# Splitting the mixer's weight pieces once and keeping both parts in DRAM, in a hybrid attention and retention layer

## The chip, the cores and the metric

The kernel runs on one core of a Trainium2 chip. The metric is device time in microseconds (us), as the median of the runs of one kernel. A core has TensorE (PE, matmuls; PEld is its weight load), VectorE (DVE), ScalarE (ACT), GpSimd (POOL) and SyncE (SP), which here only issues transfers; its 16 DMA engines are shared by all queues.

## What is computed

One step of one decoder layer, in fp32, for a prompt of 1024 tokens and a sample group of 8 sequences of 8 tokens that share the weights:

```
x = LN(alpha*x + 0.5 * swiglu(x, ffn_wi[0], ffn_wo[0]))          # D_MODEL 1024, D_FF 2816
q_a,k_a,v_a,q_r,k_r,v_r,g_r,gate_a,gate_b = split(x @ w_in)
o_a = sliding_window_attention(rope(q_a), rope(k_a), v_a)        # window 128, sinks, caches
o_r = group_norm(retention(rope(q_r), rope(k_r), v_r)) * silu(g_r)
m = sigmoid(gate_a) * (o_a @ w_br_attn) + sigmoid(gate_b) * (o_r @ w_br_ret)
x = LN(alpha*x + m @ w_o)
x = LN(alpha*x + 0.5 * swiglu(x, ffn_wi[1], ffn_wo[1]))
```

The middle four lines are the mixer. Besides the two activations the outputs are the new key and value caches and the retention states.

## The kernel before, in words

**Three parts.** The first feed-forward block runs to about 718 us, the mixer to about 1692 us, the second feed-forward block to the end. The activations stay in SBUF, partly spilled to DRAM.

**Precision.** An fp32 product is made of three matmuls (`three`, L2228 to L2232; `token_major`, L2504 and L2505, for outputs with tokens on the partitions): high part by high part, high by low, low by high. So every operand exists as a high part (rounded, type fp32r) and a low part (operand minus high part).

**The mixer's order.** `TIMELINE` (`build_timeline`, L100) is one list of stages for three token groups (G = 0, 1, 2): groups 0 and 1 have 384 prompt tokens each, group 2 has 256 and the 64 sample rows. Per retention head there are P (projection), PVQ, G and G2, TR (transposes of the rotated q and k), SKV, GN, B; then KVA and QA for the attention, gates GB and GA with the sigmoids SGB and SGA, attention units AS, EX, AP, AV, FIN, the product A with `w_br_attn`, WO (product with `w_o`), and in group 2 also the stages of the sample rows (KC reads the cached keys, SP, SV, SU). Every engine walks the same list.

**Weight pieces.** The weights of the mixer are cut into 66 pieces of 128 x 1024 (`NP_PHASE`), the same 66 in each group, so 198 in all (`NPIECES`). `STAGE_PIECES` (L167) says how many pieces a stage reads: four for P and QA, two for B, KVA and WO, else one. B and WO wait for both pieces together and free both at their end, the other stages take one after the other. A piece goes through these steps, in every group anew:

- SP loads 512 KB into one of `RAW` = 3 raw slots (`load_piece`, L721), in one transfer or a few, with rows of up to 4 KB, once the split of the piece that was there before is done.
- ACT copies it to the high part in one of `MSLOTS` = 4 slots (`split_hi`, L507 to L513), after the load and after PE has used the piece that was in the slot (`piece_used`).
- DVE computes the low part, raw minus high (`split_lo`, L515 to L520).
- PE waits for `lo_ready` and reads both parts (L2230 and L2232 the high part, L2231 the low part).

**Who sets the order.** ACT's and DVE's instruction order is written out by the code: class `Pace` (L626) puts the splits between the other work of the stages, some pieces ahead of the stage that reads them. The other work of DVE in the mixer is the rope (L1892 and on, ending in the tiles `qk` at L1940), the low parts of operands, masks and norms; that of ACT is copies out of PSUM, exponentials and sigmoids (L1282), the copy of `probT` (L1336). SP's queue holds the loads of the pieces in order (loop at L747); behind them wait the first loads of the second block's weights (`load_a`), the spills of `y` and then the rest of the second block (`ffn(1)`). The cached keys and values are loaded by POOL in group 2 (L941 and L943). The semaphores `x_loaded` belong to the input tiles of the first block and are waited for again at L1752, L1753 and L1790.

Of the kernel before, what the change touches and what calls it, by code (L numbers as in the profile page):

```python
# [13 lines left out]
P = 128  # L14
# [177 lines left out]
def slot_of(n):  # L192

    return n % MSLOTS


# [103 lines left out]
def hybrid_layer(nc, w, c, o):  # L300
# [4 lines left out]
    with ExitStack() as ctx:  # L305
# [110 lines left out]
        raw = stack("raw", RAW * D)  # L416
        w_hi4, w_lo4 = stack("w_hi4", MSLOTS * D, FR), stack("w_lo4", MSLOTS * D, FR)
        xg_hi, xg_lo = stack("xg_hi", KT * TG, FR), stack("xg_lo", KT * TG, FR)
# [9 lines left out]
        h_d = nc.dram_tensor("h_spill", (P, KD, PRODS, 512), F32, kind="Internal").ap()  # L428
        y_d = nc.dram_tensor("y_spill", (P, NT, D), F32, kind="Internal").ap()


# [11 lines left out]
        x11_loaded, x12_loaded, x21_loaded, x22_loaded, a11_loaded = x_loaded[0:4], x_loaded[4:6], x_loaded[6], x_loaded[7], x_loaded[8]  # L443
        xst_loaded = sem("xst_loaded")
        xs_done, xs_act, xs_dve = sem("xs_done"), sem("xs_act"), sem("xs_dve")
        u_hi_ready, u_dve, prod_done = sem("u_hi_ready"), sem("u_dve"), sem("prod_done")
# [41 lines left out]
        def wslot(n, lo):  # L488
            s = slot_of(n)
            return (w_lo4 if lo else w_hi4)[:, s * D:(s + 1) * D]  # L490

# [5 lines left out]
        def fr(ap):  # L497
            return ap.bitcast(F32)
# [8 lines left out]
        def split_hi(eng, n):  # L507

            eng.wait_ge(raw_loaded[n % RAW], RAW_AT[n])
            if n >= MSLOTS:  # L510
                eng.wait_ge(piece_used, n - MSLOTS + 1)
            s = n % RAW
            nc.scalar.activation(wslot(n, False), raw[:, s * D:(s + 1) * D], ACT.Copy).then_inc(hi_ready, 1)  # L513
# [112 lines left out]
        class Pace:  # L626
# [4 lines left out]
            def upto(self, n):  # L631
                while self.n < min(n, NPIECES):
                    self.split(self.eng, self.n)
                    self.n += 1
# [15 lines left out]
        def _(sp):  # L650
# [70 lines left out]
            def load_piece(n):  # L721
# [3 lines left out]
                for width, off, src in sources[n]:  # L725
                    k, cols = src.shape[1], src.shape[2]
                    dst = raw[:, s * D:(s + 1) * D].rearrange("p (k n) -> p k n", n=width)[:, 0:k, off:off + cols]
                    sp.dma_start(dst, src).then_inc(raw_loaded[s], 16)

            def load_xt(dst, feats, toks, k0, nk, landed):  # L730
                src = w["x_prompt_t"][feats * HALF + k0 * P:feats * HALF + (k0 + nk) * P, toks * HALF:(toks + 1) * HALF]
                sp.dma_start(dst[:, k0 * HALF:(k0 + nk) * HALF].rearrange("p (k c) -> p k c", k=nk),
                             src.rearrange("(k p) c -> p k c", p=P)).then_inc(landed, 16)
# [12 lines left out]
            ffn(0)  # L746
            for n in range(RAW, NPIECES):  # L747
                load_piece(n)
            sp.wait_ge(st_stored, 16 * HR)
            sp.wait_ge(out_stored, 16 * (2 + HR + 2 + 2 * DB))  # L750
# [642 lines left out]
        def _(dve):  # L1393
# [345 lines left out]
            def product_evac(f, q):  # L1739
                if q == 1:  # L1740
                    last_y.clear()
                for i in range(4):
                    src = bank(down_bank(q, i))
                    product_done(f, q, i)
                    if q == 1:
                        dve.wait_ge(tile_out, 28 * f + 4)
                        tt(part(c11, i), part(u_sum, i), src, ALU.add).then_inc(tile_out, 1)
                    elif q in (2, 5):
                        dve.wait_ge(tile_out, 28 * f + 4 * q)
                        tt(part(u_sum, i), part(u_sum, i), src, ALU.add).then_inc(tile_out, 1)  # L1750
                    elif q == 3:
                        dve.wait_ge(x_loaded[i], 32 + 16 * f)  # L1752
                        dve.wait_ge(x_loaded[i + 4], 32 + 16 * f)  # L1753
                        y_add(i, 1, ALPHA, src)
                        y_out(f, q, i + 4, 1, ALPHA, src)
                    elif q == 4:
                        y_out(f, q, i, 1, 1.0, src)
                    elif q == 6:
                        y_out(f, q, i + 4, 0, 1.0, src)
# [28 lines left out]
            def sample_out(f, half):  # L1788
                t = NT - 1
                dve.wait_ge(x_loaded[t], 32 + 16 * f)  # L1790
                dve.wait_ge(fold8_done, 2 * f + half + 1)
                stt(y_half(t, half), y_half(t, half), ALPHA, bank(7, SR), ALU.mult, ALU.add).then_inc(y8_out, 1)
# [432 lines left out]
        def _(pe):  # L2225
# [266 lines left out]
            def token_major(n, npieces, kper, width, b0, G, first=0, tile=None):  # L2492

                for i in range(first, first + npieces):
                    pe.wait_ge(lo_ready, n + i + 1 - first)
                    wh, wl = wslot(n + i - first, False), wslot(n + i - first, True)
# [17 lines left out]
            def gate(n, b, G):  # L2514
                TGn = tokens_of(G)
                pe.wait_ge(lo_ready, n + 1)
                wh, wl = wslot(n, False), wslot(n, True)
# [5 lines left out]
            for kind, G, x, n in TIMELINE:  # L2523
# [121 lines left out]
                elif kind == "B":  # L2645
                    pe.wait_ge(lo_ready, n + 2)
                    pe.wait_ge(or_lo_ready, g + 1)
# [139 lines left out]
                elif kind == "A":  # L2787
                    pe.wait_ge(lo_ready, n + 1)
                    if x == 0:
# [13 lines left out]
                elif kind == "WO":  # L2803
                    pe.wait_ge(lo_ready, n + 2)
                    pe.wait_ge(m_lo_ready, 4 * G + x + 1)
# [133 lines left out]
```

## Time and profile before

| | |
|---|---|
| median of 3 runs | 2414.72 us (2413.87 to 2414.76) |
| the profiled execution | 2422.92 us |
| its span | 2421.1 us |
| granted TensorE clock, mean | 0.994 |
| busy share PE, DVE, ACT, POOL | 98%, 69%, 38%, 9% |
| moved by DMA | 300.04 MB, 124 GB/s in the mean |

The trace is that of one execution, which took 8.2 us longer than the median. Busy shares are means over the whole span; a stretch has its own. A time in brackets behind an instruction is the idle time of its engine just before it, with what ended it. In the rows by stretch each engine has its busy microseconds and its number of instructions, then come the granted clock, the busy share of the 16 DMA engines and the GB/s they moved. Where several transfers overlap, that share can be above 1.

### The profile page before, as it was taken

What the parts mean: (1) busy time and instruction counts of PE and PEld (TensorE: products, weight loads), DVE (VectorE), ACT (ScalarE), POOL (GpSimd) and SP (SyncE); (2) the same over time, 40 slices, a digit from 0 to 9 for tenths busy, and PEclk for the clock granted to TensorE, in tenths of its full rate; (3) what the DMA queues carried; (4) which work ended last, traced back from release to release, by engine and by line L of the source; (5) the groups of instructions that cost most, each with busy time, mean ns of one, the idle gap of its engine ahead of it and who ended that gap; (6) DMA issues with size and microseconds to landing.
All of it is one profiled execution on the core that took longest, in us unless ns stands there. A gap on an engine that the chain in (4) does not pass through costs nothing.

```text
span 2421.1 us, 30917 instructions
## 1 busy us (share of the span) xinstructions
PE 2383.4 (98%) x12165; PEld 2027.9 (84%) x12165; DVE 1673.2 (69%) x2340; ACT 910.5 (38%) x1347; POOL 211.5 (9%) x297
## 2 busy tenths in 40 slices
PE   8999999999999999999999999999999999999997
PEld 7888888887888998989999778888788888888786
DVE  8666666656887657666666767577866666665788
ACT  5222222343444337443356333373422222234344
POOL 4000000000111000000100111202300000000011
PEclk9999999999999999999999999999999999999999
DMA  5222223276443334343342445534222222327643
GB/s 167 92 99 96 100 91 106 96 227 195 148 142 115 121 96 118 98 129 105 107 116 89 139 136 168 169 97 148 75 96 83 96 100 89 107 95 228 204 146 129
DMA packets 227857, 300.04 MB, mean 124 GB/s; under 512 B 14465, under 2 KB 167345, under 8 KB 224881
## 3 DMA queue, kind: packets, MB, share of 16 engines
q1 hardware_dynamic: 213392, 239.91, 32.0%
q0 software_dynamic: 13056, 56.48, 6.4%
q8 instruction: 97, 1.59, 0.3%
q10 hardware_dynamic: 1264, 1.67, 0.2%
q14 instruction: 48, 0.39, 0.0%
HBM read 243.81 MB, written 55.18 MB: 123 GB/s over the span
## 4 chain that ended last, share of the span: by engine, by line
PE 89%; DVE 6%; DMA 2%; ACT 2%; issue 1%; SPq 0%; ACTq 0%; POOL 0%; DVEq 0%
PE ps L2230 26%; PE ps L2231 25%; PE ps L2232 25%; PE ps L2349 3%; DMA b_raw<-in_ffn_wo 2%; PE ps L2438 1%; PE ps L2439 1%; DVE b_lo L1563 1%; DMA raw<-in_w_in 1%; PE ps L2604 1%; DVE w_lo L519 1%; PE ps L2739 1%; PE ps L2716 1%; DVE y L1429 1%; PE ps L2616 0%
## 5 line engine op out<-in xcount | busy, mean ns | idle before, releaser
L2230 PE MATMUL ps<-xc_hi,u_both 128*128 128x512 f32 x1240 | 485.9, 392 | 7.7 <-DVE u_both L1621 6.2
L2232 PE MATMUL ps<-xc_hi,u_both 128*128 128x512 f32 x1240 | 483.6, 390 | 0.0
L2231 PE MATMUL ps<-xc_lo,u_both 128*128 128x512 f32 x1240 | 483.5, 390 | 0.0
L519 DVE TENSOR_TENSOR w_lo<-raw,w_hi 128x1024 fp32r<-128x1024 f32 x198 | 238.8, 1221 | 103.5 <-ACT w_hi L513 103.2
L2230 PEld LDWEIGHTS ps<-xc_hi,u_both 128*128 128x128 f32 x1240 | 233.5, 188 | 56.3 <-DVE u_both L1621 6.2
L2232 PEld LDWEIGHTS ps<-xc_hi,u_both 128*128 128x128 f32 x1240 | 233.3, 188 | 49.0
L2231 PEld LDWEIGHTS ps<-xc_lo,u_both 128*128 128x128 f32 x1240 | 233.4, 188 | 47.9
L513 ACT ACTIVATE w_hi<-raw 128x1024 fp32r<-128x1024 f32 x198 | 205.4, 1054 | 163.6 <-PE ps L2232 93.5
L2230 PE MATMUL ps<-b_hi,h_hi 128*128 128x512 f32 x616 | 242.1, 393 | 4.3 <-DVE b_lo L1563 4.3
L2231 PE MATMUL ps<-b_lo,h_hi 128*128 128x512 f32 x616 | 240.5, 390 | 0.0
L2232 PE MATMUL ps<-b_hi,h_lo 128*128 128x512 f32 x616 | 240.4, 390 | 0.0
L2230 PE MATMUL ps<-w_hi,xg_hi 128*128 128x256 f32 (+1 forms) x640 | 219.7, 343 | 0.0
L2231 PE MATMUL ps<-w_lo,xg_hi 128*128 128x256 f32 (+1 forms) x640 | 215.5, 337 | 0.0
L2232 PE MATMUL ps<-w_hi,xg_lo 128*128 128x256 f32 (+1 forms) x640 | 215.4, 337 | 0.0
L1112 ACT ACTIVATE h_hi<-h_raw 128x512 fp32r<-128x512 f32 x154 | 97.3, 632 | 273.2 <-PE ps L2232 160.0
L1523 DVE TENSOR_TENSOR u_both<-wa,u_both 128x1024 fp32r<-128x1024 f32 x84 | 104.8, 1248 | 94.4 <-ACT u_both L986 94.4
L986 ACT ACTIVATE u_both<-wa 128x1024 fp32r<-128x1024 f32 (+1 forms) x89 | 93.3, 1048 | 197.6 <-PE ps L2349 100.4
L986 ACT ACTIVATE u_both<-ws 128x1024 fp32r<-128x1024 f32 x63 | 66.8, 1060 | 233.5 <-PE ps L2232 140.6
L1562 DVE TENSOR_TENSOR h_lo<-h_raw,h_hi 128x512 fp32r<-128x512 f32 x154 | 105.7, 686 | 64.3 <-ACT b_hi L986 64.0
L2230 PEld LDWEIGHTS ps<-b_hi,h_hi 128*128 128x128 f32 x616 | 116.0, 188 | 34.5 <-DVE b_lo L1563 8.5
L2232 PEld LDWEIGHTS ps<-b_hi,h_lo 128*128 128x128 f32 x616 | 116.0, 188 | 24.4
L2231 PEld LDWEIGHTS ps<-b_lo,h_hi 128*128 128x128 f32 x616 | 116.0, 188 | 23.6
(352 smaller groups left out, 4421.8 us busy)
## 6 DMA issues: line engine op xcount, KB each, us to landing
raw<-in_w_in SPq DMA_DIRECT2D x90, 512.0 KB, 3.9
wa<-in_ffn_wi SPq DMA_DIRECT2D x87, 512.0 KB, 3.8
h_raw<-h_spill SPq DMA_DIRECT2D x154, 256.0 KB, 2.9
h_spill<-tm POOLq DMA_DIRECT2D x22, 1024.0 KB, 4.2
b_raw<-in_ffn_wo SPq DMA_DIRECT2D x66, 256.0 KB, 3.9
raw<-in_w_in SPq DMA_DIRECT2D x96, 128.0 KB, 2.5
raw<-in_w_in SPq DMA_DIRECT2D x48, 256.0 KB, 3.3
raw<-in_w_br_ret SPq DMA_DIRECT2D x24, 512.0 KB, 4.4
```

Source lines behind the costliest of these rows:

```text
L513: nc.scalar.activation(wslot(n, False), raw[:, s * D:(s + 1) * D], ACT.Copy).then_inc(hi_ready, 1)
L519: nc.vector.tensor_tensor(wslot(n, True), raw[:, s * D:(s + 1) * D], fr(wslot(n, False)), ALU.subtract).then_inc(lo_ready, 1)
L986: nc.scalar.activation(dst, src, ACT.Copy).then_inc(sem_, 1)
L1112: nc.scalar.activation(h_hi[s][:], h_raw[s][:], ACT.Copy)
L1429: return nc.vector.scalar_tensor_tensor(out=out, in0=in0, scalar=scalar, in1=in1, op0=op0, op1=op1)
L1523: tt(u_lo[s][:], w_src[i][:], fr(u_hi[s][:]), ALU.subtract).then_inc(u_dve, 1)
L1562: tt(h_lo[s][:], h_raw[s][:], fr(h_hi[s][:]), ALU.subtract)
L1563: tt(b_lo[s][:], step_source(q, k, s), fr(b_hi[s][:]), ALU.subtract).then_inc(d_lo_ready, 1)
L2230: mm(out, a_hi, b_hi, start=first, stop=False)
L2231: mm(out, a_hi, b_lo, start=False, stop=False)
L2232: return mm(out, a_lo, b_hi, start=False, stop=last)
L2349: ins = mm(out, xs[:, k * P:(k + 1) * P], both[:, k], start=first and k == 0, stop=last and k == 3)
```

## The change

The splits are made in group 0 only. A slot holds both parts of a piece side by side, [high | low], 8 KB on each partition. In group 0 SP stores each split piece as 1 MB to a DRAM tensor `w_split` (`store_piece`), three loads behind; ACT's `split_hi` waits for the store of the piece that was in its slot before. In groups 1 and 2 SP fetches high and low part together, 1 MB, into the slot (`fetch_piece`) once PE has used what was there, and PE waits for `piece_fetched` in the place of `lo_ready`. `SPLIT_IN` maps a piece of group 1 or 2 to the piece of group 0 with the same weights. The stores and fetches count on eight of the semaphores `x_loaded`, so the waits of the second block on them get new values (`x_landed`).

```diff
--- before.py
+++ after.py
@@ -194,6 +194,31 @@
     return n % MSLOTS
 
 
+FIRST_USE = {(kind, x, i): n + i for kind, G, x, n in TIMELINE if G == 0 for i in range(STAGE_PIECES.get(kind, 0))}
+SPLIT_IN = {n + i: FIRST_USE[kind, x, i] for kind, G, x, n in TIMELINE
+            if kind in STAGE_PIECES and n >= NP_PHASE for i in range(STAGE_PIECES[kind])}
+
+
+def stored_count(n):
+
+    return 16 * (n // MSLOTS + 1)
+
+
+def fetched_count(n):
+
+    return 16 * sum(u % MSLOTS == n % MSLOTS for u in range(NP_PHASE, n + 1))
+
+
+def x_landed(t, f):
+
+    pieces = 0
+    if t < MSLOTS:
+        pieces = sum(n % MSLOTS == t for n in range(NP_PHASE))
+    elif t < 2 * MSLOTS:
+        pieces = sum(n % MSLOTS == t - MSLOTS for n in range(NP_PHASE, NPIECES))
+    return 32 + f * 16 * (1 + pieces)
+
+
 def block_order():
 
     return [(ci, p) for kind, p in HEAD for ci in {"E": EARLY, "L": LATE, "U": ()}[kind]]
@@ -414,7 +439,7 @@
         tA, tB = stack("tA", 512), stack("tB", 512)
         sig = stack("sig", KT * TG)
         raw = stack("raw", RAW * D)
-        w_hi4, w_lo4 = stack("w_hi4", MSLOTS * D, FR), stack("w_lo4", MSLOTS * D, FR)
+        w_both4 = stack("w_both4", MSLOTS * 2 * D, FR)
         xg_hi, xg_lo = stack("xg_hi", KT * TG, FR), stack("xg_lo", KT * TG, FR)
         ret_mask = stack("ret_mask", HR * P)
         ret_mask_s = stack("ret_mask_s", HR * SR)
@@ -427,6 +452,7 @@
 
         h_d = nc.dram_tensor("h_spill", (P, KD, PRODS, 512), F32, kind="Internal").ap()
         y_d = nc.dram_tensor("y_spill", (P, NT, D), F32, kind="Internal").ap()
+        w_d = nc.dram_tensor("w_split", (NP_PHASE, P, 2 * D), F32, kind="Internal").ap()
 
 
         raw_loaded = [sem(f"raw_loaded{i}") for i in range(RAW)]
@@ -442,6 +468,7 @@
         xb_sum, xb_done, xb_hi, xb_lo = [sem(n) for n in ("xb_sum", "xb_done", "xb_hi", "xb_lo")]
         x11_loaded, x12_loaded, x21_loaded, x22_loaded, a11_loaded = x_loaded[0:4], x_loaded[4:6], x_loaded[6], x_loaded[7], x_loaded[8]
         xst_loaded = sem("xst_loaded")
+        piece_stored, piece_fetched = x_loaded[0:MSLOTS], x_loaded[MSLOTS:2 * MSLOTS]
         xs_done, xs_act, xs_dve = sem("xs_done"), sem("xs_act"), sem("xs_dve")
         u_hi_ready, u_dve, prod_done = sem("u_hi_ready"), sem("u_dve"), sem("prod_done")
         s1_ready, q_ready, c11_ready, u3_ready, u2_ready, u1_ready, c12_ready = [
@@ -487,7 +514,14 @@
 
         def wslot(n, lo):
             s = slot_of(n)
-            return (w_lo4 if lo else w_hi4)[:, s * D:(s + 1) * D]
+            return w_both4[:, (2 * s + lo) * D:(2 * s + lo + 1) * D]
+
+        def wait_piece(eng, n):
+
+            if n < NP_PHASE:
+                eng.wait_ge(lo_ready, n + 1)
+            else:
+                eng.wait_ge(piece_fetched[slot_of(n)], 32 + fetched_count(n))
 
         def wait_affine(eng, k, t):
 
@@ -509,6 +543,7 @@
             eng.wait_ge(raw_loaded[n % RAW], RAW_AT[n])
             if n >= MSLOTS:
                 eng.wait_ge(piece_used, n - MSLOTS + 1)
+                eng.wait_ge(piece_stored[slot_of(n)], 32 + stored_count(n - MSLOTS))
             s = n % RAW
             nc.scalar.activation(wslot(n, False), raw[:, s * D:(s + 1) * D], ACT.Copy).then_inc(hi_ready, 1)
 
@@ -629,7 +664,7 @@
                 self.eng, self.split, self.n = eng, split, start
 
             def upto(self, n):
-                while self.n < min(n, NPIECES):
+                while self.n < min(n, NP_PHASE):
                     self.split(self.eng, self.n)
                     self.n += 1
 
@@ -727,6 +762,19 @@
                     dst = raw[:, s * D:(s + 1) * D].rearrange("p (k n) -> p k n", n=width)[:, 0:k, off:off + cols]
                     sp.dma_start(dst, src).then_inc(raw_loaded[s], 16)
 
+            def store_piece(n):
+                s = slot_of(n)
+                sp.wait_ge(lo_ready, n + 1)
+                sp.dma_start(w_d[n], fr(w_both4[:, 2 * s * D:2 * (s + 1) * D])).then_inc(piece_stored[s], 16)
+
+            def fetch_piece(n):
+                s, m = slot_of(n), SPLIT_IN[n]
+                sp.wait_ge(piece_used, n - MSLOTS + 1)
+                if n - MSLOTS < NP_PHASE:
+                    sp.wait_ge(piece_stored[s], 32 + stored_count(n - MSLOTS))
+                sp.wait_ge(piece_stored[slot_of(m)], 32 + stored_count(m))
+                sp.dma_start(fr(w_both4[:, 2 * s * D:2 * (s + 1) * D]), w_d[m]).then_inc(piece_fetched[s], 16)
+
             def load_xt(dst, feats, toks, k0, nk, landed):
                 src = w["x_prompt_t"][feats * HALF + k0 * P:feats * HALF + (k0 + nk) * P, toks * HALF:(toks + 1) * HALF]
                 sp.dma_start(dst[:, k0 * HALF:(k0 + nk) * HALF].rearrange("p (k c) -> p k c", k=nk),
@@ -744,8 +792,13 @@
             load_a(0, 0, 2)
             load_a(0, 0, 3)
             ffn(0)
-            for n in range(RAW, NPIECES):
+            for n in range(RAW, NP_PHASE):
                 load_piece(n)
+                store_piece(n - RAW)
+            for n in range(NP_PHASE - RAW, NP_PHASE):
+                store_piece(n)
+            for n in range(NP_PHASE, NPIECES):
+                fetch_piece(n)
             sp.wait_ge(st_stored, 16 * HR)
             sp.wait_ge(out_stored, 16 * (2 + HR + 2 + 2 * DB))
             sp.wait_ge(m_ready, KT * NG)
@@ -1749,8 +1802,8 @@
                         dve.wait_ge(tile_out, 28 * f + 4 * q)
                         tt(part(u_sum, i), part(u_sum, i), src, ALU.add).then_inc(tile_out, 1)
                     elif q == 3:
-                        dve.wait_ge(x_loaded[i], 32 + 16 * f)
-                        dve.wait_ge(x_loaded[i + 4], 32 + 16 * f)
+                        dve.wait_ge(x_loaded[i], x_landed(i, f))
+                        dve.wait_ge(x_loaded[i + 4], x_landed(i + 4, f))
                         y_add(i, 1, ALPHA, src)
                         y_out(f, q, i + 4, 1, ALPHA, src)
                     elif q == 4:
@@ -1787,7 +1840,7 @@
 
             def sample_out(f, half):
                 t = NT - 1
-                dve.wait_ge(x_loaded[t], 32 + 16 * f)
+                dve.wait_ge(x_loaded[t], x_landed(t, f))
                 dve.wait_ge(fold8_done, 2 * f + half + 1)
                 stt(y_half(t, half), y_half(t, half), ALPHA, bank(7, SR), ALU.mult, ALU.add).then_inc(y8_out, 1)
 
@@ -2492,7 +2545,7 @@
             def token_major(n, npieces, kper, width, b0, G, first=0, tile=None):
 
                 for i in range(first, first + npieces):
-                    pe.wait_ge(lo_ready, n + i + 1 - first)
+                    wait_piece(pe, n + i - first)
                     wh, wl = wslot(n + i - first, False), wslot(n + i - first, True)
                     for kk in range(kper):
                         k = i * kper + kk
@@ -2513,7 +2566,7 @@
 
             def gate(n, b, G):
                 TGn = tokens_of(G)
-                pe.wait_ge(lo_ready, n + 1)
+                wait_piece(pe, n)
                 wh, wl = wslot(n, False), wslot(n, True)
                 for k in range(KT):
                     ins = three(bank(b, n=TGn), wh[:, k * P:(k + 1) * P], wl[:, k * P:(k + 1) * P],
@@ -2643,7 +2696,8 @@
                                                       ident[0:R, 0:R])
                     ins.then_inc(t_done, 1)
                 elif kind == "B":
-                    pe.wait_ge(lo_ready, n + 2)
+                    wait_piece(pe, n)
+                    wait_piece(pe, n + 1)
                     pe.wait_ge(or_lo_ready, g + 1)
                     for f in range(KT):
                         if f in (1, 2):
@@ -2785,7 +2839,7 @@
                                          probT[:, q * P + b4 * 32:q * P + (b4 + 1) * 32], start=False, stop=(b4 == 3))
                     ins.then_inc(av_done, 1)
                 elif kind == "A":
-                    pe.wait_ge(lo_ready, n + 1)
+                    wait_piece(pe, n)
                     if x == 0:
                         pe.wait_ge(oa_lo_ready, 3 * G + 3)
                         pe.wait_ge(pT_ready, 6 * G + (6 if not last_group else 5))
@@ -2801,7 +2855,8 @@
                                         oaT_hi[:, k * TG:k * TG + TGn], oaT_lo[:, k * TG:k * TG + TGn], k == 0, k == 3)
                     ins.then_inc(piece_used, 1)
                 elif kind == "WO":
-                    pe.wait_ge(lo_ready, n + 2)
+                    wait_piece(pe, n)
+                    wait_piece(pe, n + 1)
                     pe.wait_ge(m_lo_ready, 4 * G + x + 1)
                     if x == 0:
                         pe.wait_ge(sig_done, 16 * (G + 1))
```

## Rows read from the trace of the kernel before

**Rows 1.** The page: busy time of each engine.

```profile
PE 2383.4 (98%) x12165; PEld 2027.9 (84%) x12165; DVE 1673.2 (69%) x2340; ACT 910.5 (38%) x1347; POOL 211.5 (9%) x297
```

**Rows 2.** Busy times by token group; columns: stretch, PE, PEld, DVE, ACT, POOL, clock, DMA.

```profile
718.00:1041.00 323.00, 321.82 (x1910) 293.04 (x1909) 223.99 (x359) 141.50 (x210) 19.02 (x32) 1.00 0.37 112
1041.00:1363.00 322.00, 322.00 (x1911) 293.19 (x1910) 216.78 (x349) 141.48 (x211) 18.16 (x27) 1.00 0.36 110
1363.00:1692.00 329.00, 321.21 (x2049) 275.64 (x2048) 230.20 (x397) 137.04 (x218) 52.34 (x72) 0.98 0.46 144
```

**Rows 3.** PE waits, group 2: wait <- releaser: us, times, mean us.

```profile
PE ps L2568 <- DVE qk L1940: 4.5, 1, 4.5
PE ps L2739 <- ACT probT L1336: 1.4, 2, 0.9
```

**Rows 4.** Timeline of PE, two matmuls of stage P.

```profile
722.38 0.39 PE L2230 MATMUL ps<-w_hi,xg_hi 128*128 128x512 f32 x1
722.61 0.39 PE L2231 MATMUL ps<-w_lo,xg_hi 128*128 128x512 f32 x1
```

**Rows 5.** The splits, grouped by line.

```profile
L519 DVE TENSOR_TENSOR w_lo<-raw,w_hi 128x1024 fp32r<-128x1024 f32 x198 | 238.8, 1221 | 103.5 <-ACT w_hi L513 103.2
...
L513 ACT ACTIVATE w_hi<-raw 128x1024 fp32r<-128x1024 f32 x198 | 205.4, 1054 | 163.6 <-PE ps L2232 93.5 <-DMA raw<-in_w_in 49.2 <-PE ps L2505 16.4
```

**Rows 6.** Timeline at stage TR of group 2: DVE, ACT, PE.

```profile
1380.12 1.23 DVE L519 TENSOR_TENSOR w_lo<-raw,w_hi 128x1024 fp32r<-128x1024 f32 x1 [3.91 <-ACT w_hi L513]
1381.26 0.42 DVE L1892 TENSOR_TENSOR tA<-ps,cs_ret 128x256 f32<-128x256 f32 x1
...
1379.02 1.06 ACT L513 ACTIVATE w_hi<-raw 128x1024 fp32r<-128x1024 f32 x1 [4.08 <-DMA raw<-in_w_in]
...
1385.68 0.69 PE L2568 MATMUL ps<-ident,qk 128*128 128x128 f32 x2 [4.51 <-DVE qk L1940]
```

**Rows 7.** Timeline of the last attention units: ACT, PE.

```profile
1616.21 1.05 ACT L513 ACTIVATE w_hi<-raw 128x1024 fp32r<-128x1024 f32 x1
...
1621.50 0.33 PE L2739 MATMUL ps<-probT,va 128*64 128x128 f32 x2 [0.91 <-ACT probT L1336]
```

**Rows 8.** DMA issues: size of each, median us to landing.

```profile
h_spill<-tm POOLq DMA_DIRECT2D x22, 1024.0 KB, 4.2
...
raw<-in_w_o SPq DMA_DIRECT2D x24, 512.0 KB, 3.2
...
st<-in_state_ret POOLq DMA_DIRECT2D x4, 1024.0 KB, 6.2
```

**Rows 9.** DMA share and GB/s, last two columns, in short stretches.

```profile
76.00:78.00 2.00, 2.00 (x11) 1.65 (x10) 2.00 (x2) 0.98 (x2) 0.00 (x0) 1.00 1.01 406
1378.00:1380.00 2.00, 2.00 (x19) 2.00 (x18) 0.00 (x0) 0.98 (x1) 0.00 (x0) 1.00 1.16 316
```

**Rows 10.** Timeline around WO1 of group 2: PE, ACT.

```profile
1660.07 0.30 PE L2230 MATMUL ps<-oaT_hi,w_hi 128*128 128x320 f32 x1
...
1663.58 0.39 PE L2230 MATMUL ps<-w_hi,mT_hi 128*128 128x512 f32 x1
...
1671.80 1.04 PE L2256 MATMUL ps<-ident,y 128*128 128x128 f32 x8
...
1684.33 1.09 ACT L986 ACTIVATE u_both<-wa 128x1024 fp32r<-128x1024 f32 x1
```

**Rows 11.** Timeline at the cache load of group 2: POOL, PE.

```profile
1549.48 0.89 POOL L943 DMA_DIRECT2D vc<-in_cache_v  x1
...
1557.08 1.09 PE L2703 MATMUL ps<-ident,prob 128*128 128x128 f32 x8 [1.12 <-DMA vc<-in_cache_v]
```

**Rows 12.** Timeline of a burst of splits, group 0: DVE, ACT.

```profile
905.56 3.50 DVE L519 TENSOR_TENSOR w_lo<-raw,w_hi 128x1024 fp32r<-128x1024 f32 x3 [2.40 <-ACT w_hi L513]
...
913.56 1.06 ACT L513 ACTIVATE w_hi<-raw 128x1024 fp32r<-128x1024 f32 x1 [1.83 <-DMA raw<-in_w_in]
...
925.89 0.49 ACT L1282 ACTIVATE sig<-ps 128x384 f32<-128x384 f32 x1 [2.63 <-PE ps L2232]
```

## The prediction

> **What bounds the kernel now.** I read the page first, then the busy times of the three token groups, then TensorE's waits in each group, then single stretches of the timeline, and the DMA issues last. TensorE (PE) is busy 98% of the span, VectorE (DVE) 69%, ScalarE (ACT) 38% [rows 1]. The change touches the mixer, 718 to 1692 us, where each group of 66 weight pieces takes 322 to 329 us; PE is busy 321.82 of 323 us in group 0, all 322 us of group 1 and 321.21 of 329 us in group 2 [rows 2]. TensorE's granted clock is 1.00, its 2.4 GHz level, in groups 0 and 1, and 0.98 in group 2. So groups 0 and 1 have nothing to give: a whole group has 1.2 us of PE idle or none. Group 2 has 7.8 [rows 2], and it holds the waits of the mixer: 4.5 and 1.4 us [rows 3] and 1.12 us [rows 11]. A matmul of 512 columns starts every 0.227 us [rows 4], so a piece of 18 of them (stage P) takes 4.08 us. The other stages have the same number of columns.
>
> The 198 splits cost ACT 205.4 us and DVE 238.8 us [rows 5], and 132 of them go. That is 137 us of ACT and 159 us of DVE, but both engines wait for PE here, so these microseconds are worth only what they do to PE's waits.
>
> **What the change gives, group 2.** The 4.5 us wait is the transposes of stage TR waiting for the rope on DVE. From 1376.2 DVE stood 3.91 us until ACT had split piece 138, which itself waited 4.08 us for a raw load; only after its own split of that piece, at 1380.12, did the rope begin, at 1381.26 [rows 6]. The splits go out of DVE's order, so the rope starts when its tiles are ready. PE ends stage G at 1381.2 (4.51 us before 1385.68 [rows 6]) and stage P, one piece of under 4 us earlier, near 1377.4. The rope's three tiles took 4.4 us from 1381.26 to 1385.68; only the third, with its copies 2.5 us at most of those 4.4, has to wait for the end of P, so it is done near 1379.9, before PE asks. Nothing is late next: gain 4.5 us, bounds 3.5 and 4.7.
>
> The attention units of group 2 wait for ACT: PE waits 1.4 us in two waits for the probT copy [rows 3], 0.91 of it in one, and a split of 1.05 us stands in such a turn of ACT [rows 7]. It leaves each turn, and it is longer than either wait: gain 1.7 us (the 1.4 and some 0.3 of the small waits beside it), bounds 1 and 2.5. The next thing late there is ACT's own softmax work, which I expect to be just in time.
>
> **What it costs, groups 1 and 2.** A fetch of 1 MB has 8 KB rows on both sides. The nearest row is the 1 MB store h_spill<-tm with the same rows: 4.2 us to landing; the 512 KB load of w_o, with 4 KB rows, lands in 3.2 [rows 8]. While h_spill<-tm runs, the queues move 406 GB/s at share 1.01 [rows 9], so 1 MB holds the 16 engines 1.05/0.406 = 2.6 us, and 0.5 MB of large rows 1.3. From the w_o row the fixed part is 3.2 - 1.3 = 1.9, and a fetch lands 4.5 us after its issue; the low bound is 4.2, the high bound is st<-in_state_ret with 6.2 (1 KB rows) [rows 8]. I take 4.5, since the rows are long. PE needs a piece each 4.08 us at the densest (3.5 in A3 of group 2, 1660.07 to 1663.58 [rows 10]), against 2.6 of transfer, and a slot is released three pieces, some 11 to 12 us, before its new content is read. So a fetch is hidden nearly everywhere. It is not where a stage with two pieces ends and frees both slots late. The tightest case is WO1 of group 2: A3's first matmul starts at 1660.07 [rows 10]; with one matmul time for the last of WO0, its two slots are free at 1660.3. Only one piece (A3, 3.5 us) lies between, and WO1 starts at 1663.58 [rows 10]. WO1 needs pieces 192 and 193, and 193 goes into a slot of WO0. It lands at 1660.3 + 4.5 = 1664.8: **cost 1.2 us**, bounds 0.9 and 2.9. In group 1 A3 has 384 columns for 320 (24 matmuls, 64 columns more at 2.4 GHz each: 4.2 us) and eight transposes follow it (1.0 us, as [rows 10] has them after WO1), so 5.2 us of cover: cost 0, at most 1.0 by the high bound.
>
> The second place is the cache load of group 2. The two cache transfers are issued by POOL by 1549.48, and PE already waits 1.12 us for the second [rows 11]. Stage B3 ends about a microsecond earlier and frees two slots, so SP now issues two 1 MB fetches (5.2 us of transfer) just ahead of them, where its next raw load was issued after both. Both queues then share the engines. The cache's own 1 MB is about 3 us; together 8.2, so its end moves from 1557.0 to about 1558.7, as 1549.5 + 8.2 + 1: **cost 1.7 us**. Bounds: 0 if its queue is served first, 5.2 if it is served last.
>
> **What it costs, group 0.** Load and split stay; each piece adds a store of 1 MB, 66 of them, 2.6 us of all engines each. The group now has DMA share 0.37 [rows 2], 119.5 us of 323; with 66 x 2.6 = 171 it is 291 of 323, share 0.90. On average it fits; a dense stretch asks 1.7 + 2.6 = 4.3 us per piece (1.7 is 0.52 MB at the 316 GB/s of mixed rows [rows 9]), against 4.08. What counts is the bursts. DVE ends a run of three splits at 909.1 [rows 12], one each 1.2 us, and SP now issues load 43, store 40, load 44, store 41, load 45, store 42. Counted one behind the other, load 44 lands at 914.9 instead of before the 913.56 at which its split starts, and load 45 is late by as much. PE reads piece 44 only after 925.89, where it finishes 43 [rows 12], 8 us after that split would end. The same count for every piece of the group gives lateness above 0.5 us only at pieces 4, 26 and 43 to 48, and PE has 4 us and more at each. The store of a piece lands 5 to 7 us after its low part is made, while PE is done with it 6 us later at the earliest, so the new slot wait is at most 1 us late. But DVE and ACT stand in these waits with rope and softmax work queued behind, and PE waits for those. I take **cost 0.5 us**, bounds 0 and 5.
>
> **Hand-over to the second FFN.** The last two fetches wait for WO1's end (1671.8 [rows 10]); the raw loads before waited only for splits, which DVE had some 8 us earlier, and three loads of wa and six spills of y stand behind them on SP. The first wa lands at 1671.8 + 5.2 + 1.7 + 1.9 = 1680.6 and ACT splits it at 1684.33 [rows 10]: hidden by 3.7 us. The spills guard tiles that are written after that split. Cost 0; if the cover is gone, what is left of a fetch, some 2 us.
>
> **The sum.** -4.5 - 1.7 + 1.2 + 1.7 + 0.5 = -2.8 us. The profiled execution took 2422.92 us with a span of 2421.1; the median of the three runs is 2414.72, 8.2 us less. I apply the difference to the median: 2411.9, call it **2412 us**. A measurement of this kernel tells about 0.2% from no change, 4.8 us, so this is "within".
>
> Here a rule of the Trainium skill speaks against the change. By row, 1 MB with long rows lands in 4.2 us [rows 8]. DMA: Bandwidth & Descriptors, section Bandwidth, gives 6.15 us for a 1 MB load (341 GB/s), 3.07 us per MB. By that the share of group 0 would be (119.5 + 66 x 3.07)/323 = 1.00, the edge of rival 1 below, and the fetches would land as in rival 3: an estimate of +5 us in all. The trace does not agree, by its 406 GB/s, and I go by the trace.
>
> **Rivals.** (1) *The queues of group 0 fill (slower).* Place: the raw loads behind the stores. The store is issued from SP's own queue here and shares it with short-row loads, which no row shows. At 3.2 us per MB the demand is 119.5 + 211 = 331 us against 323: the group then runs at the queues' pace, +8, plus 3 to 5 us for bursts, minus the 2.8 + 0.5 of the rest: +8 to +10, **2424 us**. It decides from about 3.05 us per MB. For it: share above 1 in stretches with mixed rows at 316 GB/s [rows 9]. Against: 8 KB rows have run at 406. The far bound is the st row, 1 MB with 1 KB rows in 6.2 us [rows 8], which less the fixed 1.9 would put the group at (119.5 + 66 x 4.3)/323 = 1.25 times its time; its rows are eight times shorter, and I leave it outside the range. Chance 0.22.
>
> (2) *All gains, no costs (faster).* -4.7 and -2.5, the cache's cost 0, WO1 hidden because a fetch lands after 4.2 us and A3 is late itself: -7, **2407.7**. For it: bursts of group 0 have slack by every row; the cache queue may be served first. Chance 0.22.
>
> (3) *Fetches land late as st does, 6.2 us.* WO1 costs 2.9 and 1.0, the cache 3, so about +1: **2415.5**, no difference to be seen. Chance 0.13.
>
> (4) *The change does not do what it says*, for instance the stores order loads behind them and DVE still waits at 1376 for something else, so that the rope stays late: +1.5, **2416**. Chance 0.05.
>
> **How the numbers follow.** The forecast has 0.38. Faster by over 0.2% holds rival 2 and the lower edge of the forecast: 0.23. Slower holds rival 1 and the upper ends of the cache and of group 0 in the forecast: 0.25. Within: 0.52. The range goes from 2407 (rival 2) to 2424 (rival 1), which leaves out less than 2 in 10.
>
> **What would show it.** In the profile after: 66 splits on ACT and DVE instead of 198; no wait for qk near 1381; PE's waits of group 1 still none; a new wait of about 1 us at the first matmul of WO1 in group 2, ended by a fetch; the wait for vc at 2 to 4 us; DMA share near 0.90 in 718 to 1041 with that stretch no longer than 325 us. Wrong would be: group 0 of 330 us or more with PE waiting for w_lo (rival 1), or PE waits ended by fetches in group 1 at stages other than WO1.

## The result

The changed kernel takes 2423.82 us (median of 6 runs, 2421.33 to 2426.78), the kernel before 2414.51 us in the same comparison: ratio 1.0036, 95% interval 1.0026 to 1.0046. That is 9.3 us slower. I had forecast 2412 us, a small gain that could not be told from no change.

The profiled execution took 2421.36 us. It is shorter than the profiled execution of before (2422.92), which stood 8.2 us above its own median; that contradiction is what the first experiment is about. From the page of the changed kernel, engines, then the three token groups as in [rows 2]:

```profile
PE 2381.7 (98%) x12165; PEld 2027.7 (84%) x12165; DVE 1522.5 (63%) x2208; ACT 782.3 (32%) x1215; POOL 197.5 (8%) x297
...
DMA packets 175407, 438.44 MB, mean 181 GB/s; under 512 B 14496, under 2 KB 95696, under 8 KB 147088
```

```profile
718.00:1041.00 323.00, 322.74 (x1914) 293.80 (x1912) 223.67 (x364) 138.59 (x206) 21.13 (x38) 1.00 0.87 327
1041.00:1363.00 322.00, 322.00 (x1911) 293.35 (x1910) 141.80 (x282) 77.29 (x144) 11.41 (x27) 1.00 0.61 216
1363.00:1692.00 329.00, 319.60 (x2044) 274.41 (x2044) 156.60 (x330) 76.80 (x156) 44.05 (x70) 0.98 0.69 248
```

DVE does 150.7 us less and ACT 128.2, and the DMA engines carry 438 MB where they carried 300. PE is busy 322.74 of 323 us in group 0 at a DMA share of 0.87, all of group 1, and 319.60 of 329 us in group 2, 1.6 us less than in [rows 2]. The splits, against [rows 5], are a third of what they were:

```profile
L554 DVE TENSOR_TENSOR w_both<-raw,w_both 128x1024 fp32r<-128x1024 f32 x66 | 79.3, 1218 | 39.1 <-ACT w_both L548 38.9
...
L548 ACT ACTIVATE w_both<-raw 128x1024 fp32r<-128x1024 f32 x66 | 68.5, 1055 | 63.6 <-DMA raw<-in_w_in 37.7 <-PE ps L2285 13.0 <-issue 10.2
```

TensorE's waits in group 2 (waited for, releaser: us, times, longest), against [rows 3]:

```profile
PE ps L2757 <- DMA vc<-in_cache_v: 7.2, 1, 7.2
PE ps L2283 <- issue: 1.5, 1, 1.5
PE ps L2695 <- ACT gs L1305: 0.4, 1, 0.4
```

The 4.5 us wait for the rope and the 1.4 us for probT are gone. In their place stands one wait of **7.2 us for the cached values**, and 1.5 us at the first matmul of WO1. The transfers around the first, as the timeline of SP's queue and of POOL shows them, with TensorE behind:

```profile
1537.05 7.99 SPq L776 DMA_DIRECT2D w_both<-w_split  x4
...
1537.33 0.90 POOL L994 DMA_DIRECT2D prob<-in_cache_k  x1 [12.29 <-PE ps L2285]
1538.22 0.89 POOL L996 DMA_DIRECT2D vc<-in_cache_v  x1
...
1551.87 1.97 PE L2757 MATMUL ps<-ident,prob 128*128 128x128 f32 x8 [7.18 <-DMA vc<-in_cache_v]
```

The transfer vc takes 13.6 us to land, from its own entry in the trace, and the four fetches 4.9 to 9.4 us:

```profile
DMA to landing us min/median/max: 13.6/13.6/13.6
```

```profile
DMA to landing us min/median/max: 4.9/8.4/9.4
```

The same stretch by time: before the wait, in it, behind it. The clock and the DMA columns are the ones to read.

```profile
1537.00:1541.00 4.00, 4.00 (x36) 4.00 (x35) 0.49 (x1) 0.00 (x0) 1.78 (x2) 1.00 0.71 240
1541.00:1552.00 11.00, 3.82 (x32) 3.62 (x32) 3.68 (x16) 0.69 (x2) 1.65 (x3) 0.87 1.02 386
1552.00:1555.50 3.50, 3.50 (x13) 3.12 (x14) 0.00 (x0) 1.02 (x1) 3.50 (x8) 0.50 0.21 63
```

While PE waits the queues are full (share 1.02). The granted clock falls from 1.00 to 0.50 (from 2.4 to 1.2 GHz) behind the idle time and stays there for about four microseconds of matmuls. The matmuls that ran at half the clock are a second cost of the same wait.

### The profile page after: what moved, and what is told of

The parts are those of the page before. It is cut to its first block, busy times and chain, and to the rows that moved or that the text cites. A ratio compares the mean times of both kernels' runs of the same rounds, so it can differ in the third digit from the quotient of the medians.

```text
span 2419.6 us, 30682 instructions
## 1 busy us (share of the span) xinstructions
PE 2381.7 (98%) x12165; PEld 2027.7 (84%) x12165; DVE 1522.5 (63%) x2208; ACT 782.3 (32%) x1215; POOL 197.5 (8%) x297
## 4 chain that ended last, share of the span: by engine, by line
PE 91%; DVE 4%; DMA 2%; POOL 1%; issue 1%; ACT 0%; SPq 0%; ACTq 0%; DVEq 0%; POOLq 0%
PE ps L2283 26%; PE ps L2285 26%; PE ps L2284 26%; PE ps L2402 3%; DMA b_raw<-in_ffn_wo 1%; DVE b_lo L1616 1%; PE ps L2492 1%; PE ps L2491 1%; PE ps L2770 1%; PE ps L2793 1%; PE ps L2657 1%; PE ps L2780 1%; DMA vc<-in_cache_v 1%; PE ps L2557 1%; PE ps L2558 1%
## 5 line engine op out<-in xcount | busy, mean ns | idle before, releaser
L2283 PE MATMUL ps<-w_both,xg_hi 128*128 128x256 f32 (+1 forms) x640 | 219.6, 343 | 0.0
L2284 PE MATMUL ps<-w_both,xg_hi 128*128 128x256 f32 (+1 forms) x640 | 215.5, 337 | 0.0
L2285 PE MATMUL ps<-w_both,xg_lo 128*128 128x256 f32 (+1 forms) x640 | 215.4, 337 | 0.0
L1039 ACT ACTIVATE u_both<-wa 128x1024 fp32r<-128x1024 f32 (+1 forms) x89 | 93.3, 1048 | 197.9 <-PE ps L2402 104.1
L1615 DVE TENSOR_TENSOR h_lo<-h_raw,h_hi 128x512 fp32r<-128x512 f32 x154 | 105.5, 685 | 63.6 <-ACT b_hi L1039 63.3
L2283 PEld LDWEIGHTS ps<-w_both,xg_hi 128*128 128x128 f32 x640 | 121.6, 190 | 14.2 <-issue 1.2
L2284 PEld LDWEIGHTS ps<-w_both,xg_hi 128*128 128x128 f32 x640 | 121.6, 190 | 12.6
```

What stands on the lines that cost most here:

```text
L1039: nc.scalar.activation(dst, src, ACT.Copy).then_inc(sem_, 1)
L1615: tt(h_lo[s][:], h_raw[s][:], fr(h_hi[s][:]), ALU.subtract)
L2283: mm(out, a_hi, b_hi, start=first, stop=False)
L2284: mm(out, a_hi, b_lo, start=False, stop=False)
L2285: return mm(out, a_lo, b_hi, start=False, stop=last)
```

## The experiments

Two theories stood at the start. **A**: the stores of group 0 cost the time (rival 1 of the prediction, whose 2424 us was met). **B**: group 0 is hidden, and the loss is in group 2: the wait for the cache, the low clock behind it and WO1, while the wait of 4.5 us that the change removed is no fixed part of the kernel before.

All kernels have the same matmuls in the same order, so their traces can be laid over each other matmul by matmul. The table gives the time from the start of one matmul to that of another in each profiled execution (the first column starts at the first matmul, the last ends at the last one), for the places that lie at 718, 1363, 1540, 1600, 1692 and 1760 us in the first profile of before. KC lies in the fourth column, the sample attention SV, A and WO1 in the fifth, the start of the second feed-forward block in the sixth.

| us | to 718 | groups 0, 1 | 1363-1540 | 1540-1600 | 1600-1692 | 1692-1760 | the rest |
|---|---|---|---|---|---|---|---|
| before, first profile | 711.9 | 645.1 | 176.9 | 60.1 | 92.0 | 68.0 | 647.7 |
| before_again | 711.2 | 644.7 | 171.8 | 59.9 | 92.3 | 68.1 | 647.8 |
| stores_only | 709.0 | 644.7 | 171.3 | 60.1 | 93.3 | 68.0 | 649.3 |
| the changed kernel | 708.4 | 644.0 | 170.3 | 68.1 | 91.8 | 69.5 | 648.2 |
| after_again | 709.5 | 644.7 | 170.3 | 68.2 | 91.7 | 69.6 | 647.6 |
| fetch_only | 709.7 | 644.3 | 170.3 | 68.3 | 91.7 | 69.6 | 647.8 |
| fetch_halves | 708.9 | 645.0 | 170.3 | 64.3 | 93.9 | 68.0 | 648.3 |
| fetch_held | 708.2 | 644.3 | 170.3 | 63.6 | 93.2 | 69.4 | 647.7 |
| cache_early | 707.8 | 644.7 | 170.3 | 58.8 | 93.2 | 69.6 | 647.9 |
| cache_early_spare | 707.5 | 644.4 | 170.3 | 58.8 | 91.5 | 70.8 | 647.9 |
| spare_again | 708.7 | 644.5 | 170.3 | 58.8 | 90.0 | 68.1 | 647.9 |

The first column varies by 4 us between executions, in code that the kernels share. A single profile's total therefore says little here; a single column says much.

### Second profiles of both kernels

No edit.

> The kernel before, unchanged, for a second profile of it. Its first profile is of an execution 8.4 us above the median, with a 4.5 us wait at the first TR of group 2 and low-clock stretches of TensorE near 574 and 1386 us. Theory A (the stores of group 0 cost the 9.3 us) says nothing of this run beyond 2414.5 us. Theory B (the 4.5 us wait is no fixed part of the kernel before, so its removal gained little, and group 2 lost some 9 us at the cache load and WO1) expects an execution near 2414.5 us without the 4.5 us wait or with at most 1 us of it, and no low clock behind it.

> The changed kernel, unchanged, for a second profile. Both theories expect 2421 to 2427 us. Theory A expects PE waits of 3 us or more in group 0 (718 to 1041) in an execution that takes 2424 or more. Theory B expects under 1 us there and again 6 to 8 us for the cached values at KC in group 2, with a low granted clock right behind it.

Measured: before_again 2416.19 us (ratio 0.9998, 0.9990 to 1.0007), after_again 2422.92 us (1.0030, 1.0018 to 1.0043). In before_again the TR of group 2 waits 1.3 us where the first profile had 4.5, and KC waits 0.9:

```profile
1381.30 1.22 PE L2568 MATMUL ps<-ident,qk 128*128 128x128 f32 x6 [1.30 <-DVE qk L1940]
...
1550.55 1.09 PE L2703 MATMUL ps<-ident,prob 128*128 128x128 f32 x8 [0.89 <-DMA vc<-in_cache_v]
```

In the first profile of before the same place is followed by the low clock, which neither the rows nor the sum of the prediction had:

```profile
1384.00:1388.00 4.00, 2.32 (x8) 1.43 (x9) 3.57 (x9) 1.07 (x3) 0.00 (x0) 0.50 0.17 58
1388.00:1392.00 4.00, 4.00 (x27) 4.00 (x27) 1.65 (x2) 2.61 (x4) 0.00 (x0) 0.70 0.52 140
```

The column 1363 to 1540 says it whole: 176.9 us in that one execution, 171.8 in the other, 170.3 with the fetches. The change gains 1.5 us there, not 4.5 with what lies behind it. after_again repeats the loss, with its low clock right behind:

```profile
1553.59 1.97 PE L2757 MATMUL ps<-ident,prob 128*128 128x128 f32 x8 [7.11 <-DMA vc<-in_cache_v]
```

```profile
1554.00:1558.00 4.00, 4.00 (x15) 3.43 (x14) 0.00 (x0) 1.02 (x1) 4.00 (x9) 0.50 0.18 51
1718.00:1722.00 4.00, 3.94 (x16) 3.03 (x15) 3.01 (x7) 1.35 (x4) 0.00 (x0) 0.57 0.30 66
```

Theory B was right on both, but for 1.3 us of the wait at TR where it had allowed 1; group 0 shows 0.6 us of PE waits at the most. The second row there is a smaller loss that neither theory had: at 1718 to 1722, where the second feed-forward block starts with waits that both kernels have, the clock falls to 0.57; before_again comes to this place 4.6 us earlier, and its clock stays at 1.00 there and behind it:

```profile
1714.00:1718.00 4.00, 4.00 (x18) 3.26 (x19) 3.17 (x6) 1.21 (x4) 0.00 (x0) 1.00 0.32 70
1718.00:1722.00 4.00, 4.00 (x19) 3.31 (x18) 2.87 (x4) 2.42 (x3) 0.00 (x0) 1.00 0.43 133
```

### Each half of the change alone

stores_only keeps all 198 loads and splits and adds the stores; fetch_only stores four pieces and makes all the fetches of the changed kernel, each of one of these four, so groups 1 and 2 go without the other weights.

```diff
 # stores_only
-            for n in range(RAW, NP_PHASE):
+            for n in range(RAW, NPIECES):
                 load_piece(n)
-                store_piece(n - RAW)
+                if n - RAW < NP_PHASE:
+                    store_piece(n - RAW)
...
 # fetch_only
-                store_piece(n - RAW)
+                if n - RAW < MSLOTS:
+                    store_piece(n - RAW)
...
-                s, m = slot_of(n), SPLIT_IN[n]
+                s, m = slot_of(n), SPLIT_IN[n] % MSLOTS
```

> The kernel before with its 198 loads and splits, and with the 66 stores of 1 MB in group 0 on top, which nothing reads. Theory A expects +7 to +10 us against the kernel before, B 0 to +2, with a DMA share near 0.87 in group 0 in both.

> The changed kernel with stores for the first 4 pieces alone; groups 1 and 2 fetch as many times as before, each time one of these 4 pieces, so the weights of groups 1 and 2 are wrong ones. Theory A expects -2 to +1 us against the kernel before, B +7 to +9, with the wait for the cached values of 6 to 8 us at KC in its profile.

Measured: stores_only 2419.70 us (ratio 1.0014, 1.0006 to 1.0023, so +3.4 with 1.4 to 5.6), fetch_only 2422.81 us (1.0030, 1.0018 to 1.0041). The fetches alone make the loss of after_again; A is refuted. Yet stores_only came out above B's 2 us. Its profiled execution, at 2416.91 us, is 2.8 us below that median, so it need not hold what the timed runs have. Group 0 takes 322.8 us in it, against 322.7 in before_again; what is longer in its row of the table stands behind 1600 (1.0 us up to 1692, 1.5 us in the last column), and 2.2 us less stand up to 718. These are its PE waits and its row for the whole group:

```profile
PE ps L2619 <- DVE qk L1991: 0.3, 1, 0.3
PE ps L2643 <- ACT gs L1303: 0.2, 1, 0.2
```

```profile
718.00:1041.00 323.00, 322.50 (x1911) 293.35 (x1910) 225.41 (x365) 142.62 (x210) 20.08 (x35) 1.00 0.88 325
```

To see whether the stores cost something that profiles don't catch, cache_early_few_stores (below) leaves them out again.

### What the wait for the cache is made of

fetch_halves splits each fetch in two, so that its rows are 4 KB; fetch_held makes SP wait for the cache before it fetches the first piece of QA in group 2.

```diff
 # fetch_halves
-                sp.dma_start(fr(w_both4[:, 2 * s * D:2 * (s + 1) * D]), w_d[m]).then_inc(piece_fetched[s], 16)
+                for i in range(2):
+                    sp.dma_start(fr(w_both4[:, (2 * s + i) * D:(2 * s + i + 1) * D]), w_d[m][:, i * D:(i + 1) * D]).then_inc(piece_fetched[s], 16)
...
 # fetch_held
+                if n == HELD_N:
+                    sp.wait_ge(cache_loaded, 32)
                 sp.wait_ge(piece_used, n - MSLOTS + 1)
```

> The changed kernel, with each fetch made as two transfers of 512 KB with 4 KB rows (high part, low part) instead of one with 8 KB rows. Theory D (the engines take turns between the queues packet by packet, so that a 512-byte packet of the cache stands behind an 8 KB one) expects the wait for the cache at 2.5 to 4.5 us. Theory E (the cache only shares the bandwidth with the fetches issued before it, whatever their rows) expects 6.5 to 7.5 us, as in the changed kernel.

> The changed kernel, with SP waiting until the cache has landed before it fetches the first piece of QA in group 2, so that the order of the two is turned round. Both D and E expect the cache to land 6 us or more sooner and the wait at KC at 0 to 1 us, and in its place a wait of 1 to 4 us for the fetch at the first matmul of QA: 4 to 7 us less than the changed kernel.

Measured: fetch_halves 2422.45 us (ratio 1.0030, 1.0018 to 1.0042), fetch_held 2418.39 us (1.0012, 1.0003 to 1.0021). With rows half as long, and the same bytes, vc lands in 10.1 us and the wait is 3.6; held back, it lands in 5.4 us and PE waits 3.0 us for the fetch instead. PE's wait and the transfer's entry, for the one and the other:

```profile
PE ps L2758 <- DMA vc<-in_cache_v: 3.6, 1, 3.6
```

```profile
DMA to landing us min/median/max: 10.1/10.1/10.1
```

```profile
PE ps L2286 <- DMA w_both<-w_split: 3.0, 1, 3.0
```

```profile
DMA to landing us min/median/max: 5.4/5.4/5.4
```

vc lands in 5.4 us with no fetch beside it, in 10.1 beside 4 KB rows and in 13.6 beside 8 KB rows. (In fetch_halves the last half megabyte is issued just behind vc and not ahead of it; at [rows 9]'s 406 GB/s that is worth 1.3 us of the 3.5.) The packets of the two queues say why; each line has their number, the MB and the share of the engines. q0 is POOL's queue with the two caches, q1 is SP's. First the changed kernel from 1537 to 1541.8 and from 1541.8 to 1551, then fetch_halves from 1542.9 to 1549.1, then fetch_held from 1539 to 1543.3; the last three are the stretches in which the caches move:

```profile
q1 hardware_dynamic: 175, 1.30, 76.2%
```

```profile
q1 hardware_dynamic: 331, 2.45, 72.4%
q0 software_dynamic: 282, 1.05, 30.0%
```

```profile
q0 software_dynamic: 285, 1.05, 53.4%
q1 hardware_dynamic: 317, 1.13, 49.4%
```

```profile
DMA packets 288, 1.05 MB, mean 244 GB/s; under 512 B 32, under 2 KB 32, under 8 KB 288
```

The 1.05 MB of the caches are 256 packets of 4 KB and some very small ones. So theory D's 512 bytes, which are the rows of the cache in DRAM, are not the packets that the trace has. Its turns are there: while the caches move, the other queue gets through about as many packets (331 for 282, and 317 for 285), whether they hold 8 KB or 4 KB. The caches then take 9.2 us beside 8 KB packets, 6.2 beside 4 KB ones and 4.3 alone. That is how the Trainium skill has it (DMA: Bandwidth & Descriptors, section Queues, rings and completion order: an engine takes turns between its queues, a packet at a time); these runs agree, and I had not weighed that rule. It does not explain all: in the changed kernel the first packet of the caches comes 4.5 us after their issue at 1537.33 (in the first line POOL's queue moves nothing), in fetch_halves 4.2 us, in fetch_held 1.6. These 2.9 us between the first and the last hardly depend on the packets' length, and no run shows what they are made of.

In fetch_halves 4 us less stand in the column of KC, but 2 us more behind 1600, where WO1 now waits 2.0 us, and almost nothing in the median. Its profiled execution took 2419.67 us, 2.8 below its median; what the other executions have more is not known.

### The cache out of the way

The raw slots are idle after group 0. cache_early loads the cached keys and values into two of them in group 1; cache_early_spare also fetches the second piece of WO1 in group 2 there, before WO0 ends.

```diff
 # cache_early
-                elif kind == "KVA" and G == NG - 1:
-
-                    pool.wait_ge(piece_used, n)
-                    pool.wait_ge(st_stored, 16 * HR)
-                    pool.dma_start(prob[:, 0:1024].rearrange("p (b e) -> p b e", b=DB),
+                elif kind == "P" and G == 1 and x == 1:
+                    pool.wait_ge(lo_ready, NP_PHASE)
+                    pool.dma_start(raw[:, 0:1024].rearrange("p (b e) -> p b e", b=DB),
...
 # cache_early_spare, besides; SPARE_N is the second piece of that WO1
-                sp.wait_ge(piece_used, n - MSLOTS + 1)
+                sp.wait_ge(piece_used, n - MSLOTS + (n != SPARE_N))
...
+                dst = spare[:] if n == SPARE_N else w_both4[:, 2 * s * D:2 * (s + 1) * D]
```

> The changed kernel, with the cached keys and values of group 2 loaded in group 1 into two of the raw slots, which nothing uses after the last split of group 0; KC and SV read them there. Theory B (the wait for the cache is the loss) expects the wait of 7.1 us at KC and the low clock behind it gone: -8 to -9 us against the changed kernel, so 2413 to 2416 us, the kernel before within 0.1%. If what was lost is lost to the traffic in general (theory A), it stays above 2419.

> As cache_early, and the second piece of WO1 in group 2 is fetched into the same raw region once PE is through with piece 188, instead of waiting for WO0 to free its slot. Theory B expects the 1.5 us gap at the first matmul of WO1 gone and 1 to 2 us less than cache_early, so 2411 to 2414.5 us; if the gap is not the fetch, it stays and the time is that of cache_early.

> cache_early_spare unchanged, for a second measurement: 2410 to 2413 us and below the kernel before by more than the uncertainty; if the first one was a lucky set, 2414 to 2416.

Measured: cache_early 2414.85 us (ratio 0.9994, 0.9984 to 1.0003), 8.1 us below after_again; cache_early_spare 2411.18 us (0.9985, 0.9976 to 0.9994), and again 2411.76 us (0.9984, 0.9975 to 0.9992). PE's waits from 1540 to 1692, first cache_early, then cache_early_spare:

```profile
PE ps L2281 <- issue: 1.4, 1, 1.4
PE ps L2307 <- DVE xc_lo L1511: 1.2, 1, 1.2
```

```profile
PE ps L2312 <- DVE xc_lo L1516: 1.2, 1, 1.2
```

No wait at KC, 58.8 us in its column against 68.2, 1.1 less than before. The gap at WO1, which the profile names "issue", goes with the earlier fetch, so it was the fetch. The version with both beats both kernels: 3.8 to 4.3 us below the kernel before, 11.7 below the changed one.

### The stores: how much, and how close to the edge

cache_early_few_stores is cache_early with stores for four pieces alone, and with the fetches of fetch_only. stores_and_half makes every second store twice, to a second tensor.

```diff
 # stores_and_half
                 sp.dma_start(w_d[n], fr(w_both4[:, 2 * s * D:2 * (s + 1) * D])).then_inc(piece_stored[s], 16)
+                if n % 2:
+                    sp.dma_start(w_e[n], fr(w_both4[:, 2 * s * D:2 * (s + 1) * D])).then_inc(piece_stored[s], 16)
```

> cache_early with stores for the first 4 pieces alone (the fetches of groups 1 and 2 read these 4, so their weights are wrong ones). If the 62 stores left out cost what stores_only showed in its timed runs (+3.4 us, though its profile showed no wait for them), this takes 3 to 4 us less than cache_early, 2411 to 2412. If the stores are hidden and that difference was spread, it takes what cache_early takes within 1.5 us, 2413.5 to 2416.5.

> The changed kernel with every second store of group 0 made twice, 99 MB in the place of 66. By the profile of the changed kernel a stored MB holds the engines (0.87 - 0.37) x 323 / 66 = 2.45 us, so 33 more ask for 81 us where 42 are left: group 0 should take 30 to 50 us longer, with its DMA share at 1.0 and PE waiting for w_both. If the loads are kept on time by something else than the free share (the stores giving way to them), it takes under 10 us longer.

Measured: cache_early_few_stores 2413.72 us (ratio 0.9993, 0.9984 to 1.0002), cache_early 0.9994: the 62 stores cost nothing that can be told, though each of these intervals reaches some 2 us to either side. In the profiles group 0 takes 322.4 us without them and 322.8 with them. What stores_only showed above that is not explained; its 11 runs spread from 2415.1 to 2424.4, and it keeps the loads and splits of groups 1 and 2, so the two are not the same comparison. It stays open. stores_and_half took 2462.53 us (1.0188, 1.0175 to 1.0202); group 0 takes 357.7 us for 322.7, 35 more. The rows of the stretch and its largest PE waits:

```profile
718.00:1041.00 323.00, 302.62 (x1777) 275.50 (x1776) 200.35 (x330) 133.88 (x201) 19.02 (x32) 0.97 1.01 392
1041.00:1080.00 39.00, 33.77 (x150) 27.67 (x149) 22.94 (x34) 5.33 (x6) 3.15 (x9) 0.91 0.94 387
```

```profile
PE ps L2286 <- DVE racc L2105: 7.8, 2, 5.9
PE ps L2286 <- DMA w_both<-w_split: 5.2, 1, 5.2
PE ps L2286 <- DVE racc L2103: 3.8, 2, 3.6
```

So the mechanism of rival 1 is real, and it was not reached: with 33 more MB the share is 1.01 and the excess falls on PE, mostly through DVE work queued behind late splits (racc), as the prediction said of that queue.

## Why the prediction was wrong

**The outcome.** I forecast 2412, not to be told from no change; it is 2423.8, slower. That the range held it was luck: it did so by rival 1, whose mechanism was not at work here. Step by step, against before_again:

**The gain at TR** (forecast 4.5 us, bounds 3.5 and 4.7). The mechanism was right: no split stands before the rope now. The size came from one execution in which raw piece 138 landed late. The column 1363 to 1540 shows 1.5 us against the second profile. The warning stood in my own sum: an execution 8.2 us above its median. I subtracted a gain measured in it from the median, as if the median contained it ("I apply the difference to the median"). That step failed, by 3 us. The first profile's excess lies at just such places: 5.1 us in this column alone.

**The cache** (forecast cost 1.7 us, bounds 0 and 5.2). This failed most, and it is the term that turned the sign. The wait went from 0.9 or 1.1 to 7.1 or 7.2, so it cost 6.2, above my upper bound, and the column 1540 to 1600 lost 8.3. I saw the place and both transfers. Three things were missing. I counted the two fetches issued with the cache and not the two that follow as KVA frees its slots, at 1540.9 and 1544.7 in the trace of after; so "served last" was 5.2 us of others' transfer where it could be 10.4. I let the queues share by bytes, where they take turns by packets, and a fetch's packet is twice as long as one of the cache. And I gave no price to the clock: 7 us of idle time were followed by about 4 us at 0.50, 2 us of work lost. A low clock behind the 4.5 us wait stood in the trace of before. Of the time to landing, 2.9 us passed before the cache's first packet, and their cause is open.

**probT** (gain 1.7): gone from PE's waits. The column 1600 to 1692 gained 0.5 with WO1's wait in it, so 2.0: right. **WO1** (cost 1.2, bounds 0.9 and 2.9): 1.5, right, in the place named. **Fetches** (landing in 4.5 us): median 4.9 us.

**Group 0** (cost 0.5): 322.7 us in both; cost 0. Share 0.87 for 0.90 forecast, so a stored MB holds the engines 2.45 us, where I had 2.6 from the 406 GB/s of [rows 9]. The estimate of 3.07 us per MB, from the 341 GB/s that the Trainium skill gives for 1 MB (DMA: Bandwidth & Descriptors, section Bandwidth), would have given a share of 1.00; the trace does not agree, here as before. **Group 1**: nothing, as forecast. So what the prediction named as signs held for the 66 splits, for qk, WO1, group 1 and group 0 (323 us long, share 0.87), and failed for vc, where it had 2 to 4 us.

**Hand-over** (cost 0): the first loads are in time, but the column 1692 to 1760 lost 1.5 us by the low clock near 1718. It fell in most of the kernels with fetches, though not in fetch_halves or spare_again, and in none of three without. What sets it off there was not tested. The columns from 1363 to 1760 give 8.3 + 1.5 - 1.5 - 0.5 = +7.8 us (the first column varies by itself and is left out); the medians gave +7.5 for after_again (2422.92 against 2415.41 in its comparison) and +9.3 in the first one.

## What to carry to other kernels

Freeing an engine that is not the bound buys nothing by itself: 151 us less of DVE were worth 3.5 us of PE's waits, and the traffic that replaced them cost 6.2 us in one wait, at the one transfer with the smaller packets and no slack, and 2 us more by the clock behind it. When a change fills the queues, list every small transfer issued among the new big ones, count all of those that are issued until it lands, and move it to a quiet place; here that alone took the loss away (2414.85 us, no different from before), and with one more fetch made earlier there was a gain of 4 us. And take a second profile before a single wait is counted as a gain, above all when the profiled execution is slower than the median.

## What the runs showed of the hardware

A load of 512 KB, whose rows in DRAM are 512 bytes and whose packets are 4 KB, landed in 5.4 us beside its twin alone, in 10.1 us beside transfers with 4 KB rows and in 13.6 us beside 8 KB rows of the same total size. The two queues moved about as many packets each, so the queue with the long ones got most of the bandwidth (2.45 MB against 1.05 in 9.2 us); its own landings there were 4.9 to 9.4 us. TensorE's granted clock fell to 0.50 within or behind waits of 4.5 and 7 us and stayed there for about 4 us of matmuls; it fell to 0.50 behind the waits of 3.6 us (fetch_halves) and 3.0 us (fetch_held) too, and stayed at 1.00 behind those of 0.9 and 1.3 us in before_again. The profiles also show it low once in the sample attention, with no wait of that size ahead of it and in both kernels (SV, 0.50 from 1628 to 1632 in the changed kernel and in before_again, with PE busy for all of these 4 us). And 99 MB of stores beside the loads of group 0 kept the queues at a share of 1.01 for 323 us, at 392 GB/s.
